# Convolution units of the first mixer: fp32 and split weight units in turn

## What is computed

```python
u = rmsnorm(h, g_mix)
q, k, v, z, xbc, dt_raw, g_a, g_s = split(u @ w_in)
q, k = rope(q), rope(k)
attn = softmax(window_mask(q @ k.T) with sinks) @ v       # 16 heads of 64
xbc = silu(causal_depthwise_conv(xbc, conv_w, 4 taps) + conv_b)   # 3072 channels
y = ssd_chunked(xs * dt, ..., bm, cm)                     # from xbc and dt
```

## Time and profile before

| | us |
|---|---|
| three runs, median | 2766.43 |
| three runs, lowest and highest | 2765.12, 2769.42 |
| profiled execution, its own time | 2766.32 |
| its span, first to last instruction | 2764.2 |
| PE busy in the span | 2721.0 (98%) |
| DVE busy | 1945.6 (70%) |
| ACT busy | 1405.1 (51%) |
| POOL busy | 101.6 (4%) |

### The profile page before, as it was taken

The page is one execution under the profiler, slowest core; times in us unless marked ns, Lnnn a source line. Parts: engine busy times, 40 slices in busy tenths (PEclk is TensorE's granted clock), DMA queues, the critical chain, the costliest instruction groups (busy, mean ns, idle before and its releaser), DMA issues.

```text
span 2764.2 us, 41613 instructions
## 1 busy us (share of the span) xinstructions
PE 2721.0 (98%) x16606; PEld 2389.4 (86%) x16606; DVE 1945.6 (70%) x2922; ACT 1405.1 (51%) x2084; POOL 101.6 (4%) x189
## 2 busy tenths in 40 slices
PE   8999999999999999999999999999999999999998
PEld 7888888888888888888888899988888888888887
DVE  7448777757677775677656778876788775677764
ACT  6345555544455554455445551256655553455543
POOL 1320000000000000000000000000000000000000
PEclk9999999999999999999999999998999999999999
DMA  7457556555668878877656566862355555555554
GB/s 241 134 179 239 174 183 197 184 183 186 200 219 292 283 276 301 290 282 275 202 186 210 182 192 232 279 235 97 133 177 196 190 190 192 180 193 190 183 194 141
DMA packets 166609, 573.19 MB, mean 207 GB/s; under 512 B 19872, under 2 KB 26736, under 8 KB 165904
## 3 DMA queue, kind: packets, MB, share of 16 engines
q1 hardware_dynamic: 151216, 521.86, 56.6%
q0 software_dynamic: 15056, 48.65, 4.8%
q10 hardware_dynamic: 144, 0.01, 0.0%
HBM read 530.86 MB, written 38.90 MB: 206 GB/s over the span
## 4 chain that ended last, share of the span: by engine, by line
PE 90%; DVE 5%; ACT 2%; DMA 1%; issue 1%; POOL 0%; DVEq 0%; SPq 0%; ACTq 0%; POOLq 0%
PE PS L946 89%; DVE wl L1910 2%; DVE CC L1918 1%; DMA raw<-in_w_in 1%; ACT wh L1367 1%; PE PS L1282 0%; DVE H L1910 0%; DVE SQA L1910 0%; DMA XC<-KTC 0%; DVE QT L1910 0%; ACT TB L1367 0%; DMA raw<-in_w_up 0%; DVE Z L1910 0%; DVE RB L1969 0%; PE PS L1109 0%
## 5 line engine op out<-in xcount | busy, mean ns | idle before, releaser
L1910 DVE TENSOR_TENSOR wl<-raw,wh 128x1024 fp32r<-128x1024 f32 (+1 forms) x880 | 1029.8, 1195 | 442.9 <-ACT wh L1367 441.0
L1367 ACT ACTIVATE wh<-raw 128x1024 fp32r<-128x1024 f32 (+1 forms) x880 | 885.9, 1031 | 518.6 <-PE PS L946 418.5
L946 PE MATMUL PS<-CHt,wh 128*128 128x512 f32 x2816 | 886.1, 396 | 2.4 <-DVE wl L1910 2.4
L946 PE MATMUL PS<-BIGt,wh 128*128 128x512 f32 (+1 forms) x2816 | 758.5, 357 | 2.3 <-DVE wl L1910 1.3
L946 PEld LDWEIGHTS PS<-CHt,wl 128*128 128x128 f32 x2816 | 529.0, 188 | 124.8
L946 PE MATMUL PS<-AHt,wh 128*128 128x512 f32 (+1 forms) x1984 | 602.9, 385 | 12.6 <-DVE wl L1910 9.4
L946 PE MATMUL PS<-CHt,wl 128*128 128x256 f32 x2816 | 553.5, 278 | 0.0
L946 PEld LDWEIGHTS PS<-BIGt,wl 128*128 128x128 f32 x2304 | 436.6, 189 | 79.1 <-issue 0.2
L946 PE MATMUL PS<-BIGt,wl 128*128 128x256 f32 x2304 | 499.4, 280 | 0.0
L946 PEld LDWEIGHTS PS<-BIGt,wh 128*128 128x128 f32 x2816 | 436.9, 191 | 7.2 <-issue 4.7
L946 PEld LDWEIGHTS PS<-CHt,wh 128*128 128x128 f32 x2816 | 429.3, 189 | 2.9 <-issue 2.7
(11 more groups left out here) (307 smaller groups left out, 1648.3 us busy)
## 6 DMA issues: line engine op xcount, KB each, us to landing
raw<-in_w_up SPq DMA_DIRECT2D x264, 512.0 KB, 5.0
raw<-in_w_in SPq DMA_DIRECT2D x200, 512.0 KB, 4.1
raw<-in_w_down SPq DMA_DIRECT2D x132, 512.0 KB, 4.3
raw<-in_w_gate SPq DMA_DIRECT2D x88, 512.0 KB, 5.4
raw<-in_w_down SPq DMA_DIRECT2D x56, 384.0 KB, 3.6
raw<-in_w_ssd_br SPq DMA_DIRECT2D x32, 512.0 KB, 4.5
raw<-in_w_o SPq DMA_DIRECT2D x32, 512.0 KB, 4.3
PKR<-in_w_in SPq DMA_DIRECT2D x32, 512.0 KB, 5.1
```

The costliest lines, as they stand in the source:

```text
L946: return e.matmul(o, l, r, start=start, stop=stop, skip_group_check=True)
L1367: return e.activation(o, x, f, **k)
L1910: return e.tensor_tensor(o, x, y, op)
```

## The change

`FULL_XBC` becomes a tuple of the full units. Units 0, 2, 4 and 6 stay full, units 1, 3 and 5 become split.

```diff
-FULL_XBC = 7
+FULL_XBC = (0, 2, 4, 6)
...
     for i in range(12):
         add("w_in", 0, 16, 3584 + 256 * i, "U1", "ev_xbc", i,
-            mode="full" if i < FULL_XBC else "turn",
+            mode="full" if i in FULL_XBC else "turn",
...
-                e.wait_ge(sub_done.sem, end_of("ev_xbc", FULL_XBC - 1))
+                e.wait_ge(sub_done.sem, end_of("ev_xbc", FULL_XBC[-1]))
```

More of the change, by code:

```diff
@@ L191, in all_units @@
     for i in range(12):
-        add("w_in", 0, 16, 3584 + 256 * i, "U1", "ev_xbc", i, mode="full" if i < FULL_XBC else "turn",
+        add("w_in", 0, 16, 3584 + 256 * i, "U1", "ev_xbc", i, mode="full" if i in FULL_XBC else "turn",
             gens2=([2] if i == 0 else []) + [stage("conv4", i, 5)] + ([stage("dt", 0, 2)] if i == 0 else [1] if i == 11 else []))
```

## The result

The changed kernel takes 2770.44 us (median of 20 runs, 2768.52 to 2772.81), the kernel before, beside it, 2765.77 us (20 runs, 2763.04 to 2769.42). The ratio is 1.0018, 95% interval 1.0012 to 1.0024: slower by about 4.7 us, a small difference but clear of the scatter, and above the range of the prediction (2767.0). The profiled execution took 2770.84 us, with a span of 2769.0 against 2764.2.

What follows compares the result with a forecast made beforehand. The prediction took PE, busy throughout from 87.40 to 204.85 us, as the bound: 8.1 us saved less 3.4 us of waits, net 4.7 us, gives 2761.6 us against the profiled 2766.32; range 2757.8 to 2767.0.

Steps and rivals of the forecast that it cites:

- PE is the bound, the others have room: Between 87.40 and 204.85 us: PE busy for all 117.45 us, DVE with 51.67 and ACT with 44.91 us of work.
- 12 x 0.68 = 8.1 us saved on PE: Units 1, 3, 5: twelve blocks become split, each taking PE 2.88 us in place of 3.56, 8.1 us less on the path.
- The estimate from the rule of the Trainium skill: Split blocks of units 1, 3, 5: three of four fp32 passes, 2.67 us a block, 10.7 us saved, 2759.1 us in all.
- Waits of 3.4 us: PE beside units 1 and 3: five waits for splits, scalings and attention steps, 0.2 + 1.5 + 0.3 + 0.7 + 0.7 us; none in unit 5.
- From block 54 on the order is the old one ... so the gain is kept: After the changed stretch: PE again busy throughout in the old order, so the net 4.7 us stay to the end.
- nothing there hangs on a clock time: From block 54 on: arriving earlier changes nothing, one of the reasons given for keeping the 4.7 us gain.
- Late splits, slower: Units 1 to 5: six splits directly behind exponentials or scalings each expose 2.28 us, 13.7 in all; +5.6, 2771.9 us; chance 0.07.
- No waits: Units 1 to 5: the queues run a little ahead and all 8.1 us come through, 2758.2 us; chance 0.25.
- The clock rival: Units 1 to 5: waits of 5 us and two falls of the granted clock, 3.4 us, leave 2766.6 us, no change; chance 0.18.
- A gain before block 54 that is gone at the end: Whole kernel: listed among the signs that would show the forecast wrong; no size given.

## Why the prediction was wrong

- **PE is the bound, the others have room: right** for four full units. The same share argument would have let me split all units but the first, and that version is the slowest in the table: there is room by share of time, but not in the order.
- **12 x 0.68 = 8.1 us saved on PE: nearly.** PE's busy time in the stretch fell from 117.45 to 110.39 us, by 7.1. A pair of split blocks takes 5.78 us, 2.89 each, as forecast from unit 7. A block that stands alone between two attention phases takes more, 2.99 for the one from 115.71 to 118.70. Ten of the twelve stand alone and take 2.96 on the mean (2.90 to 3.07), 0.08 more than forecast; that is 0.8 of the missing 1.0 us. The estimate from the rule of the Trainium skill (FP8 and Floating Point Precision, section TensorE Precision Notes) was 2.67 for a block. No block here reaches it.
- **Waits of 3.4 us: right in kind, a little large.** 0, 1.33, 0.23, 0.31 and 0.51 us where I had 0.2, 1.5, 0.3, 0.7 and 0.7, in the same places with the same releasers (the first of them didn't come), none in unit 5. Block 54 starts at 200.19; I had said 200.1. The two errors, 1.0 us each with opposite signs, cancel, so that agreement is luck.
- **"From block 54 on the order is the old one ... so the gain is kept": the step that failed.** The order is the old one; the banks are not. The banks alone, on the kernel before, cost 0.33% (8 us), more than the gain of 4.7 us; in the changed kernel PE waits 7.59 us at the first query unit and 2.04 us at the first output unit. Nothing in my views could show it as a wait of the kernel before, but the code could: the counter `gb` goes up by two for a split unit and by one for a full one, and it is never reset. I read the list of instructions for order and left out the destination. I also wrote "nothing there hangs on a clock time"; between 1780 and 1790 us DVE is busy for 9.90 of 10 us in the changed kernel and was as full before, and PE passed that place only because it didn't have to wait for it.
- **The rivals.** "Late splits, slower" had the right sign and nearly the right time, 2771.9, by a mechanism that was not at work here: no split of the six was exposed with its 2.28 us (the longest wait was 1.33). With 0, 3 and 6 full ACT and DVE do fall behind, but there PE waits mostly for steps of the attention and not for splits. "No waits" had 2.4 us against it. The clock rival named the wrong place: the clock stayed at 1.00 in the stretch and fell behind the waits at 1790 and 2052 us.
- **What would show it.** "A gain before block 54 that is gone at the end" stood in the list of what would be wrong, and that is what came.

## What to carry to other kernels

A change of how many banks, buffers or semaphores one unit takes is a change of the whole program, if a running counter deals them out: compare the destination of every later unit, above all where a stage with another number of banks begins. A bank taken twice in a row cost nothing where the engine that empties it was in time (the first output unit of the kernel before follows a unit in the same bank 0, and PE doesn't wait), and the whole lateness where it was late; here 7.6 us at one border and 10.7 at another, against a gain of 4.7. And on an engine that works in order, ask which short step stands behind a split that itself waits, not how busy the engine is.

## What the runs showed of the hardware

The granted clock after a pause is not settled by the length of the pause. At a wait among the products of `CHt` around 2050 us all versions have the same work ahead, and in the two shown here PE had been busy without a break since the output unit at 1972 us. After 1.81 us of waiting the changed kernel was at 0.59 over the next 4 us, that is mostly at 1.2 GHz; in the version with only the bank behind the heads moved it was at 1.00 after 1.80 us:

```profile
2052.73:2056.73 4.00, 4.00 (x14) 3.38 (x15) 3.96 (x5) 1.92 (x3) 0.00 (x0) 0.59 0.76 228
```

```profile
2052.70:2056.70 4.00, 4.00 (x23) 3.52 (x24) 3.96 (x5) 1.92 (x3) 0.00 (x0) 1.00 0.74 259
```

In the kernel before it stayed at 1.00 after 2.42 us. What follows takes 704.10 us with the drop and 702.53 without, 1.6 us. Of the twelve kernels profiled four have the drop (after 1.81, 1.86, 1.96 and 2.09 us) and eight don't (after 1.56 to 2.42 us). Of the 4.8 us between the two spans these 1.6 may therefore not belong to the change at all; single profiles can't tell, and I made no run for it. After the long wait the drop is there and was not foreseen at this place: 0.50 in the 4 us behind 1790.

```profile
1790.00:1794.00 4.00, 3.89 (x18) 3.89 (x19) 3.27 (x10) 0.63 (x1) 0.00 (x0) 0.50 0.02 6
```
